# Opening of a two-block transformer kernel: loads, modulation, bounds and first norm in one stage, a ring of 12 modulation slots, every eighth group multiplied as plain fp32

## The chip, the cores and the metric

The kernel runs on one core of one Trainium2 chip. The metric is the device time of one execution in microseconds (us); lower is better. The kernel before took 4742.59 us (median of 3 runs, 4739.91 to 4749.90).

## What is computed

Two transformer blocks, one after the other, on 256 tokens of 1024 features in fp32. The first has two layers. Each layer modulates its normalised input by shift, scale and gate vectors which are products of a conditioning vector with a large weight matrix. These products, for the token stream and for a context stream, are the work that the change touches:

```python
cond_x = jax.nn.silu(c)
cond_c = jax.nn.silu(c_ctx)
for l in range(DEPTH):                                  # DEPTH = 2
    mod_x = (cond_x @ w_mod[l] + b_mod[l])[:, None, :]  # w_mod[l]: 1024 x 6144
    mod_c = (cond_c @ w_mod[l] + b_mod[l])[None, None, :]
    ...
    hc = modulate(rms_norm(xc, norm1_g[l]), sh1c, sc1c)
    ...
    hx = modulate(rms_norm(x, norm1_g[l]), sh1x, sc1x)
```

Here `modulate(h, shift, scale)` is `h * (1 + scale) + shift` and `rms_norm` divides by the root of the mean square over the features. `lower`, a softmax over the small `lb_logits`, gives the bounds of the forget gates. What follows in each layer (a gated linear recurrence with a short convolution, then a layer of 16384 experts of which 128 are gathered per token, then the second block) is the same in both kernels.

## The kernel before

Everything is written out by hand for each engine: a stage is a block in which SyncE (SP), TensorE (PE), ScalarE (ACT), VectorE (DVE) and GpSimd (POOL) each run their own list in order, and semaphores tie them. Between two stages all engines meet (`stage`, L124). The first stages, up to the first projection, are these:

1. **load** (L2761): SP issues the small tables, the constants, the tokens (`X`, 2 MB), and the first six weight units; it waits for all but the units.
2. **cond** (L577): ACT makes silu of both conditioning vectors and its rounded high part; DVE makes the low part (`parts`).
3. **modulate** (L597): the modulation weights of both layers are 96 units of 128x1024 fp32 (512 KB each), in 24 groups of four. They pass through the ring `k.ring` of 6 slots (`RING`). fp32 precision is reached with a faster matmul format by splitting each unit: ACT casts it to a high part (`w_high`, L645), DVE subtracts it from the unit to get a low part (`w_low`, L665), which also frees the ring slot: SP waits for it and then loads unit u + 6. For a group, PE multiplies 4 stationary columns (`parts`: high and low of two conditioning vectors) by 512 moving columns, 8 k-tiles x 2 parts = 16 matmuls (L629). ACT copies the 4x512 result out of PSUM (`rows`, L650), PE turns it by four small matmuls against the constant `fold` (`turn`, L617), and DVE adds the bias (`take`, L658). PE turns group g-1 after it has multiplied group g; ACT copies group g-1 after it has cast group g; DVE takes group g-2 after the subtractions of group g. `w_high` and `w_low` have room for two groups, so ACT may cast group g only when PE has multiplied group g-2:

```python
act.wait_ge(s.multiplied, g - 1)     # ahead of the casts of group g
act.wait_ge(s.multiplied, g)         # ahead of the copy of group g-1
```

4. **bounds** (L672): a load of the activation tables, then a chain of small DVE operations with one ACT exponential, on 128x8 and 128x16 values.
5. **w_in of layer 0** (`stream` L335, called from `token_mixer_1` L1134): first the norm. ACT squares the 8 tiles of `X` (L233), DVE adds them (7 additions, L261), PE sums over partitions with a matrix of ones (L254, with 16 and 14 filling matmuls before and after, L163), ACT takes Ln and Exp (L238, L240). Then tile by tile DVE scales (L268), ACT applies gain and shift (L248) and makes the high part (L457), DVE the low part (L501), and PE multiplies with the first weight unit (L416). From the second unit on the stage streams weight units, 24 matmuls each.

`Norm` (L212) holds the norm's steps for each engine. `Order` (L147) makes DVE wait for each of its own results.

Of the kernel before, what the change touches and what calls it, by code (L numbers as in the profile page):

```python
# [15 lines left out]
P = 128  # L16
D = 1024
# [156 lines left out]
def plan_weights(a):  # L174
# [7 lines left out]
    for l in range(DEPTH):  # L182
        chunks(a.w_mod[l], range(48))
    for l in range(DEPTH):
# [27 lines left out]
class Norm:  # L212
# [5 lines left out]
    def __init__(self, k, x, T, gain, shift, out):  # L218
        self.k, self.x, self.T, self.gain, self.shift, self.out = k, x, T, gain, shift, out
# [10 lines left out]

    def act_squares(self, act, s):
        for c in range(KD):
            act.activation(self.sq[:, c, :], self.x[:, c, :], ACT.Square).then_inc(s.squares, 1)  # L233
# [101 lines left out]
def stream(k, name, outs, x, evict, signals="", gain=None, norm=None, split_x=None, ahead=True, tables=False,  # L335
# [32 lines left out]
    with ExitStack() as es, stage(k, name, "x_high x_low took squares added sum logged root scaled shifted " + signals) as (block, s):  # L368
# [8 lines left out]
        if norm is not None:  # L377
            norm.place(es)
# [17 lines left out]
        def _(pe):  # L396
            steps = None
            if norm is not None:
                fill(k, pe, 16, 0)
                norm.pe_sum(pe, s)  # L400
                fill(k, pe, 14, 0)
            elif split_x is None:
                fill(k, pe, 4, 0)
            for u, (c, j) in enumerate(unit_of):
# [17 lines left out]
                if u == LAG:  # L422
                    if gain is not None or norm is not None:
                        pe.wait_ge(s.logged, 1)
# [9 lines left out]
        def _(act):  # L434
# [11 lines left out]
            if norm is not None:  # L446
                norm.act_squares(act, s)
            make(first + 1)
            if norm is not None:
# [28 lines left out]
        def _(dve):  # L478
# [11 lines left out]
            if norm is not None:  # L490
                norm.dve_add(dve, s)
            make(first + 1)
            if norm is not None:
                norm.dve_scale(dve, s, 0)
            if split_x is None:
                for t in range(KT):
                    if norm is not None and t + 1 < KT:
# [74 lines left out]
def modulation(k):  # L572

    with ExitStack() as es:
        cond = sbuf(k, es, "cond", [P, KD, 2])
        parts = sbuf(k, es, "parts", [P, KD, 2, 2], F32R)
        with stage(k, "cond", "done high") as (block, s):  # L577
            @block.scalar
            def _(act):

                act.activation(cond[:, :, 0], k.small("c_ctx"), ACT.Silu)
                act.activation(cond[:, :, 1], k.small("c"), ACT.Silu).then_inc(s.done, 1)
                act.wait_ge(s.done, 1)
                act.copy(parts[:, :, 0, :], cond[:, :, :]).then_inc(s.high, 1)

            @block.vector
            def _(dve):
                dve.wait_ge(s.high, 1)
                dve.tensor_tensor(parts[:, :, 1, :], cond[:, :, :], parts[:, :, 0, :].bitcast(F32), ALU.subtract)

        n_units, first = DEPTH * 48, k.used
        n_groups = n_units // 4
        k.used += n_units
        with stage(k, "modulate", "w_high w_low took turned added multiplied") as (block, s):  # L597
            rows = sbuf(k, es, "rows", [4, 2, 4 * P])
            w_high, w_low = (sbuf(k, es, n, [P, 2, 4, D], F32R) for n in ("w_high", "w_low"))
            fold = k.const("fold")[0:4, :]  # L600

            @block.sync
            def _(sp):
                for u in range(n_units):

                    sp.wait_ge(s.w_low, u + 1)
                    load_unit(k, sp, u + RING)

            @block.tensor
            def _(pe):  # L610
                def turn(g):

                    pe.wait_ge(s.took, g + 1)
                    if g >= 2:
                        pe.wait_ge(s.added, g - 1)
                    for i in range(4):
                        last = pe.matmul(k.bank[4 + g % 2][:, 2 * i:2 * i + 2], rows[:, g % 2, i * P:(i + 1) * P], fold,  # L617
                                         start=True, stop=True)
                    last.then_inc(s.turned, 1)

                for g in range(n_groups):
                    if g >= 4:

                        pe.wait_ge(s.took, g - 3)

                    pe.wait_ge(s.w_low, 4 * g + 4)
                    for t in range(KD):
                        for n_pass, w in enumerate((w_high, w_low)):
                            last = pe.matmul(k.bank[g % 4][0:4, :], parts[:, t, :, :].rearrange("p a b -> p (a b)"),  # L629
                                             w[:, g % 2, :, t * P:(t + 1) * P], start=(t == 0 and n_pass == 0), stop=(t == KD - 1 and n_pass == 1))  # L630
                    last.then_inc(s.multiplied, 1)
                    if g >= 1:
                        turn(g - 1)
                turn(n_groups - 1)

            @block.scalar
            def _(act):
                for g in range(n_groups + 1):
                    for u in range(4 * g, min(4 * g + 4, n_units)):
                        if g >= 2:  # L640

                            act.wait_ge(s.multiplied, g - 1)

                        act.wait_ge(k.landed[u % RING], 16 * (u // RING + 1))
                        act.copy(w_high[:, g % 2, u % 4, :], k.ring[:, u % RING, :]).then_inc(s.w_high, 1)  # L645
                    if g >= 1:
                        act.wait_ge(s.multiplied, g)
                        if g >= 3:
                            act.wait_ge(s.turned, g - 2)
# [2212 lines left out]
```

## Time and profile before

| what | value |
|---|---|
| median of 3 runs | 4742.59 us (4739.91 to 4749.90) |
| span of the profiled execution, first to last instruction | 4744.7 us |
| execution time of that same run | none is given beside its span |
| mean granted TensorE clock | 0.962 of full speed |
| busy share of the span: PE, DVE, ACT, POOL | 84%, 62%, 42%, 21% |
| modulate: first to last split matmul | 22.42 to 152.57 us |
| first matmul of the first projection | 171.62 us |

The span is the one measure in which the trace can be summed; the median lies 2.1 us under it. A matmul group is written line, engine, operation, output<-inputs. In rows of the timeline the first number is the start, the second how long the merged instructions took together. Idle time in square brackets is that of the engine just before, with what ended it.

### The profile page before, as it was taken

To read this page: it belongs to the slowest core of one execution; us is meant where nothing else is said; L and a number is where in the kernel's file an instruction comes from. 1 tells how busy PE (TensorE), PEld (TensorE's weight loads), DVE (VectorE), ACT (ScalarE), POOL (GpSimd) and SP (SyncE) were. 2 spreads that over 40 slices of the span, in tenths; PEclk is the share of its full clock that TensorE was granted. 3 is DMA by queue.
4 is the path that set the end of the run, shared out by engine and by line. 5 is a ranking of instruction groups with operands and counts; after the bars stand their busy time and mean duration, and the time that the engine had idled before them with its cause. 6 is when DMAs were issued, how large, how long until landed. Compare 5 with 4: busy or idle time off the path is not lost. (4 is left out here: it accounts for less than half of the span.)

```text
span 4744.7 us, 58234 instructions
## 1 busy us (share of the span) xinstructions
PE 3992.4 (84%) x20895; PEld 2891.1 (61%) x20895; DVE 2951.7 (62%) x6036; ACT 1989.0 (42%) x4530; POOL 987.2 (21%) x914
## 2 busy tenths in 40 slices
PE   7895897777777777796877777899989999999999
PEld 3685663223232232396632222789989988998899
DVE  7646556676666666566766665546566574565565
ACT  7635323333333333454333333544434353444453
POOL 0004114444444444203244443000010003000000
PEclk9997999999999999998999999989999998999999
DMA  9420149999999999631699999315534540254244
GB/s 371 168 89 1 54 178 421 421 421 418 413 415 413 414 415 415 261 131 39 256 421 422 419 412 410 111 54 171 160 99 147 162 147 18 77 168 148 81 152 151
DMA packets 205745, 1143.73 MB, mean 241 GB/s; under 512 B 24064, under 2 KB 25600, under 8 KB 106640
## 3 DMA queue, kind: packets, MB, share of 16 engines
q0 software_dynamic: 110592, 805.36, 41.1%
q1 hardware_dynamic: 94864, 334.65, 21.5%
q8 instruction: 166, 2.72, 0.2%
q14 instruction: 123, 1.01, 0.1%
HBM read 1138.87 MB, written 1.05 MB: 240 GB/s over the span
## 5 line engine op out<-in xcount | busy, mean ns | idle before, releaser
L1396 PE MATMUL bank<-rows,diag 128*128 128x512 f32 x2304 | 1080.8, 614 | 375.6 <-ACT diag L1455 375.6
L416 PE MATMUL bank<-x_high,w_high 128*128 128x272 f32 (+3 forms) x3560 | 1105.9, 311 | 20.5 <-DVE x_low L501 18.7
L416 PE MATMUL bank<-x_high,w_low 128*128 128x272 f32 (+3 forms) x3560 | 1086.3, 305 | 0.0
L416 PE MATMUL bank<-x_low,w_high 128*128 128x272 f32 (+3 forms) x3560 | 1084.2, 305 | 0.0
L1396 PEld LDWEIGHTS bank<-rows,diag 128*128 128x128 f32 x2304 | 422.4, 193 | 1027.4 <-ACT diag L1455 594.7
L1502 DVE CUSTOM_DVE_ANT_0 junk<-rows,hT 128x1024 f32<-128x1024 f32 x576 | 705.4, 1225 | 410.2 <-DMA rows<-in_peer_uv,expert 406.0
L443 ACT CAST w_high<-ring 128x1024 fp32r<-128x1024 f32 (+2 forms) x541 | 554.9, 1029 | 872.5 <-PE bank L416 859.4
L486 DVE TENSOR_TENSOR w_low<-ring,w_high 128x1024 fp32r<-128x1024 f32 (+2 forms) x541 | 647.3, 1198 | 334.5 <-ACT w_high L443 333.1
L1352 POOL DMA_INDIRECT rows<-in_peer_uv,expert x576 | 614.4, 1067 | 1108.8 <-PE bank L1396 806.7
L416 PEld LDWEIGHTS bank<-x_high,w_high 128*128 128x128 f32 (+1 forms) x3560 | 675.6, 190 | 64.0 <-DVE x_low L501 23.1
L416 PEld LDWEIGHTS bank<-x_low,w_high 128*128 128x128 f32 (+1 forms) x3560 | 676.6, 190 | 22.8
L416 PEld LDWEIGHTS bank<-x_high,w_low 128*128 128x128 f32 (+1 forms) x3560 | 675.3, 190 | 23.3
L1444 ACT ACTIVATE gelu<-products 128x2 f32<-128x2 f32 x384 | 78.1, 203 | 1277.7 <-DVE products L1502 1277.7
L1396 PE MATMUL bank<-H,diag 128*128 128x512 f32 x768 | 358.1, 609 | 120.1 <-ACT diag L1455 120.1
L1502 DVE CUSTOM_DVE_ANT_0 junk<-H,hT 128x1024 f32<-128x1024 f32 x192 | 235.3, 1225 | 211.5 <-DMA H<-in_peer_uv,expert 211.5
L1396 PEld LDWEIGHTS bank<-H,diag 128*128 128x128 f32 x768 | 139.5, 191 | 337.7 <-ACT diag L1455 197.2
L1455 ACT ACTIVATE diag<-const,weighed 128x128 f32<-128x128 f32 x768 | 266.8, 394 | 0.6 <-ACT weighed L1449 0.4
L1352 POOL DMA_INDIRECT H<-in_peer_uv,expert x192 | 190.0, 990 | 281.5 <-PE bank L1396 277.1
L416 PE MATMUL bank<-hidden_high,w_high 128*128 128x272 f32 (+1 forms) x704 | 202.2, 287 | 1.5 <-PEq L130 1.5
L416 PE MATMUL bank<-hidden_high,w_low 128*128 128x272 f32 (+1 forms) x704 | 201.7, 286 | 0.0
L416 PE MATMUL bank<-hidden_low,w_high 128*128 128x272 f32 (+1 forms) x704 | 201.5, 286 | 0.0
L1449 ACT ACTIVATE weighed<-gelu,weight 128x1 f32<-128x1 f32 x768 | 184.4, 287 | 15.5
(399 smaller groups left out, 4794.7 us busy)
## 6 DMA issues: line engine op xcount, KB each, us to landing
ring<-in_w_gate_up SPq DMA_DIRECT2D x176, 512.0 KB, 3.5
ring<-in_w_mod SPq DMA_DIRECT2D x96, 512.0 KB, 5.5
ring<-in_w_in SPq DMA_DIRECT2D x64, 512.0 KB, 3.5
ring<-in_fox_w_in SPq DMA_DIRECT2D x64, 512.0 KB, 3.5
ring<-in_w_down SPq DMA_DIRECT2D x64, 512.0 KB, 3.5
ring<-in_peer_wq SPq DMA_DIRECT2D x32, 512.0 KB, 3.5
ring<-in_gdn_w_in SPq DMA_DIRECT2D x32, 512.0 KB, 3.5
ring<-in_w_down SPq DMA_DIRECT2D x32, 384.0 KB, 3.7
```

Of the source, the lines that this page charges most:

```text
L416: last = pe.matmul(k.bank[c % outs_banks][0:m, 0:nt], w[:, slot, cols], xx[:, t, t0:t0 + nt], start=(t == 0 and n_pass == 0), stop=(t == K ...
L443: act.copy(k.w_high[:, made % SPLIT, 0:width(made)], k.ring[:, made % RING, 0:width(made)]).then_inc(k.high_made, 1)
L486: dve.tensor_tensor(k.w_low[:, made % SPLIT, 0:n], k.ring[:, made % RING, 0:n], k.w_high[:, made % SPLIT, 0:n].bitcast(F32), ALU.subtract) ...
L1352: pool.indirect_dma_start(slot(n), None, table, bass.IndirectOffsetOnAxis(ap=expert[:, i % 2, e:e + 1], axis=0)).then_inc(landed[n % SLOTS ...
L1396: last = pe.matmul(k.bank[2 * (i % 2) + half][:, :], diag[:, n % 4, :], slot(n)[:, D + half * 512:D + (half + 1) * 512], start=(e == 0), s ...
L1444: act.activation(gelu[:, pair % 4, :], products[:, i % 2, e:e + 2], ACT.Gelu).then_inc(s.gelu, 1)
L1449: act.mul(weighed[:, pair % 4, j:j + 1], gelu[:, pair % 4, j:j + 1], weight[:, i % 2, e + j:e + j + 1]).then_inc(s.weighed, 1)
L1455: act.mul(diag[:, (n + j) % 4, :], k.ident, weighed[:, pair % 4, j:j + 1]).then_inc(s.diag, 1)
L1502: dve.tensor_tensor_reduce(junk[:, n % 2, :], slot(n)[:, 0:D], hT[:, i, :], 1.0, 0.0, ALU.mult, ALU.add, products[:, i % 2, e:e + 1]).then ...
```

## The change

The first four stages and the norm of the first projection become one stage, `opening`.

- SP issues the table `small`, then 12 modulation units into a ring of their own (`MOD_RING`), then the other five tables, then the tokens, then the remaining 84 units, and at last the first six units of the projection weights into `k.ring`.
- Groups 7, 15 and 23 are `whole`: no cast and no subtraction; PE multiplies them straight out of the ring by `cond` in fp32, 8 matmuls of 2 stationary and 512 moving columns, and their slots are freed when the group is multiplied. The other 21 groups are split as before, with the same two places for `w_high` and `w_low`.
- PE waits for all five tables before its first group. ACT squares two tiles of `X` after each of the groups 3 to 6 and takes the root after group 11's place; DVE adds the squares after the subtractions of group 8, scales two tiles in each of the groups 13 to 16, and makes the bounds at group 1; PE sums at group 9.
- The projection stage then starts with gain and shift; its filling matmuls are 10.

The diff, without the removed stages (they stand in the kernel above), the small operations on 128x8 values, and the plumbing:

```diff
-            act.wait_ge(s.scaled, c + 1)
+            if not self.scaled:
+                act.wait_ge(s.scaled, c + 1)
...
-        if norm is not None:
+        rooted = norm is not None and not norm.scaled
+        if rooted:
             norm.place(es)
...
-            if norm is not None:
+            if rooted:
                 fill(k, pe, 16, 0)
                 norm.pe_sum(pe, s)
                 fill(k, pe, 14, 0)
+            elif norm is not None:
+                fill(k, pe, 10, 0)
...
+MOD_RING = 12
+WHOLE_EVERY = 8
+def opening(k, a, norm):
+    n_units = DEPTH * 48
+    n_groups = n_units // 4
+    whole = lambda g: g % WHOLE_EVERY == WHOLE_EVERY - 1
+    wholes = lambda g: g // WHOLE_EVERY
+    halved = lambda u: u + 1 - 4 * wholes(u // 4)
+    side = lambda g, first, last: range(max(0, KD * (g - first) // (last - first)), min(KD, KD * (g - first + 1) // (last - first)))
+    signals = ("small tables tokens landed0 landed1 landed2 landed3 landed4 landed5 landed6 landed7 landed8 landed9 landed10 landed11 "
+               "done high parts w_high w_low took turned biased multiplied order exps subs ")
+    with ExitStack() as es, stage(k, "open", signals + norm.signals) as (block, s):
+        landed = [s.landed0, s.landed1, s.landed2, s.landed3, s.landed4, s.landed5, s.landed6, s.landed7, s.landed8, s.landed9,
+                  s.landed10, s.landed11]
...
+        @block.sync
+        def _(sp):
+            def load(u):
+                sp.dma_start(ring[:, u % MOD_RING, :], a.w_mod[u // 48][u % 48]).then_inc(landed[u % MOD_RING], 16)
+            sp.dma_start(k.small_sb[:, :], a.small).then_inc(s.small, 16)
+            for u in range(MOD_RING):
+                load(u)
+            for dst, src in ((k.const_sb[:, :], a.const), (k.both[:, :, :], a.both), (k.fox_b[:, :], a.fox_b),
+                             (k.gdn_ab[:, :], a.gdn_ab), (k.alpha[:, :], a.gla_w_alpha2_2[0])):
+                sp.dma_start(dst, src).then_inc(s.tables, 16)
+            sp.dma_start(k.X[:, :, :], a.tokens).then_inc(s.tokens, 16)
+            for u in range(n_units - MOD_RING):
+                if whole(u // 4):
+                    sp.wait_ge(s.multiplied, u // 4 + 1)
+                else:
+                    sp.wait_ge(s.w_low, halved(u))
+                load(u + MOD_RING)
+            for u in range(RING):
+                load_unit(k, sp, u)
+        @block.tensor
+        def _(pe):
+            def turn(g):
+                pe.wait_ge(s.took, g + 1)
+                if g >= 2:
+                    pe.wait_ge(s.biased, g - 1)
+                n = 2 if whole(g) else 4
+                for i in range(4):
+                    last = pe.matmul(k.bank[4 + g % 2][:, 2 * i:2 * i + 2], rows[0:n, g % 2, i * P:(i + 1) * P], fold[0:n, :],
+                                     start=True, stop=True)
+                last.then_inc(s.turned, 1)
+            pe.wait_ge(s.parts, 1)
+            pe.wait_ge(s.tables, 16 * 5)
+            for g in range(n_groups):
+                if g >= 4:
+                    pe.wait_ge(s.took, g - 3)
+                if whole(g):
+                    at = 4 * g % MOD_RING
+                    for u in range(4 * g, 4 * g + 4):
+                        pe.wait_ge(landed[u % MOD_RING], 16 * (u // MOD_RING + 1))
+                    for t in range(KD):
+                        last = pe.matmul(k.bank[g % 4][0:2, :], cond[:, t, :], ring[:, at:at + 4, t * P:(t + 1) * P],
+                                         start=(t == 0), stop=(t == KD - 1))
+                else:
+                    pe.wait_ge(s.w_low, halved(4 * g + 3))
                     for t in range(KD):
                         for n_pass, w in enumerate((w_high, w_low)):
                             last = pe.matmul(k.bank[g % 4][0:4, :], parts[:, t, :, :].rearrange("p a b -> p (a b)"),
+                                             w[:, split_group(g) % 2, :, t * P:(t + 1) * P], start=(t == 0 and n_pass == 0),
+                                             stop=(t == KD - 1 and n_pass == 1))
+                last.then_inc(s.multiplied, 1)
+                if g >= 1:
+                    turn(g - 1)
+                if g == 9:
+                    norm.pe_sum(pe, s)
+            turn(n_groups - 1)
+        @block.scalar
+        def _(act):
...
+            before = {}
+            for g in range(n_groups):
+                if not whole(g):
+                    before[split_group(g)] = g
+            for g in range(n_groups + 1):
+                if g < n_groups and not whole(g):
+                    j = split_group(g)
                     for u in range(4 * g, 4 * g + 4):
+                        if j >= 2:
+                            act.wait_ge(s.multiplied, before[j - 2] + 1)
+                        act.wait_ge(landed[u % MOD_RING], 16 * (u // MOD_RING + 1))
+                        act.copy(w_high[:, j % 2, u % 4, :], ring[:, u % MOD_RING, :]).then_inc(s.w_high, 1)
+                if g >= 1:
+                    act.wait_ge(s.multiplied, g)
+                    if g >= 3:
+                        act.wait_ge(s.turned, g - 2)
+                    n = 2 if whole(g - 1) else 4
+                    act.copy(rows[0:n, (g - 1) % 2, :], k.bank[(g - 1) % 4][0:n, :]).then_inc(s.took, 1)
+                if g == 3:
+                    act.wait_ge(s.tokens, 16)
+                for c in side(g, 3, 7):
+                    norm.act_square(act, s, c)
+                if g == 11:
+                    norm.act_root(act, s)
         @block.vector
         def _(dve):
             order = Order(dve, s.order)
+            lb = k.small("lb_logits").rearrange("p (l n) -> p l n", l=DEPTH)
+            def take(g):
+                dve.wait_ge(s.turned, g + 1)
+                l, c = divmod(4 * g, 48)
+                bias = k.small("b_mod")[:, 4 * g:4 * g + 4].unsqueeze(2).broadcast_to([P, 4, 2])
+                dve.tensor_tensor(k.mods[:, l, c:c + 4, :], k.bank[4 + g % 2][:, 0:8].rearrange("p (c q) -> p c q", q=2),
+                                  bias, ALU.add).then_inc(s.biased, 1)
                 for n, (scale0, name) in enumerate(((8, "norm1_g"), (32, "norm2_g"))):
+                    if c == scale0 + 4:
+                        dve.wait_ge(s.biased, g + 1)
+                        gain = k.small(name)[:, l * KD:(l + 1) * KD].unsqueeze(2).broadcast_to([P, KD, 2])
+                        dve.scalar_tensor_tensor(out=k.gain[:, l, n, :, :], in0=k.mods[:, l, scale0:scale0 + KD, :],
+                                                 scalar=1.0, in1=gain, op0=ALU.add, op1=ALU.mult)
...
+            dve.wait_ge(s.high, 1)
+            dve.tensor_tensor(parts[:, :, 1, :], cond[:, :, :], parts[:, :, 0, :].bitcast(F32), ALU.subtract).then_inc(s.parts, 1)
+            for g in range(n_groups):
+                if not whole(g):
+                    j = split_group(g)
+                    for u in range(4 * g, 4 * g + 4):
+                        dve.wait_ge(s.w_high, halved(u))
+                        dve.tensor_tensor(w_low[:, j % 2, u % 4, :], ring[:, u % MOD_RING, :], w_high[:, j % 2, u % 4, :].bitcast(F32),
+                                          ALU.subtract).then_inc(s.w_low, 1)
+                if g >= 2:
+                    take(g - 2)
+                if g == 1:
+                    dve.wait_ge(s.exps, 1)
...
+                if g == 8:
+                    norm.dve_add(dve, s)
+                for c in side(g, 13, 17):
+                    norm.dve_scale(dve, s, c)
+            take(n_groups - 2)
+            take(n_groups - 1)
 def first_block(k, a):
-    modulation(k)
...
-            token_mixer_1(k, l, Norm(k, k.X[:, :, :], TWO, gain(0), shift(0), k.H[:, :, :]))
+            token_mixer_1(k, l, Norm(k, k.X[:, :, :], TWO, gain(0), shift(0), k.H[:, :, :], scaled=(l == 0)))
...
+        norm = Norm(k, k.X[:, :, :], TWO, None, (), k.H[:, :, :])
+        with ExitStack() as first:
+            norm.place(first)
+            opening(k, a, norm)
```

Four pieces of the engines' order show the move. The names are the lines of each kernel.

PE around group 7. Before:

```order
L629 MATMUL bank<-w_low,parts 4x512
L617 MATMUL bank<-const,rows 128x2 x4
L629 MATMUL bank<-w_high,parts 4x512
L629 MATMUL bank<-w_low,parts 4x512
L629 MATMUL bank<-w_high,parts 4x512
```

and now (L651 is the multiplication of a whole group, L636 the turn of the group before it):

```order
L657 MATMUL bank<-w_low,parts 4x512
L636 MATMUL bank<-const,rows 128x2 x4
L651 MATMUL bank<-mod_ring,cond 2x512 x8
L636 MATMUL bank<-const,rows 128x2 x4
L657 MATMUL bank<-w_high,parts 4x512
L657 MATMUL bank<-w_low,parts 4x512
```

In place of 16 split matmuls stand 8 of plain fp32, and the turn of group 6 comes behind them.

DVE in groups 6 to 9. Before, subtractions and one bias addition alternate:

```order
L665 TENSOR_TENSOR w_low<-ring,w_high 128x1024 x4
L658 TENSOR_TENSOR mods<-bank,small 128x8
L665 TENSOR_TENSOR w_low<-ring,w_high 128x1024 x4
L658 TENSOR_TENSOR mods<-bank,small 128x8
L665 TENSOR_TENSOR w_low<-ring,w_high 128x1024 x4
```

and now:

```order
L736 TENSOR_TENSOR w_low<-mod_ring,w_high 128x1024 x4
L713 TENSOR_TENSOR mods<-bank,small 128x8 x2
L736 TENSOR_TENSOR w_low<-mod_ring,w_high 128x1024 x4
L713 TENSOR_TENSOR mods<-bank,small 128x8
L263 TENSOR_TENSOR total<-H 128x512
L263 TENSOR_TENSOR total<-total,H 128x512 x6
L736 TENSOR_TENSOR w_low<-mod_ring,w_high 128x1024 x4
L713 TENSOR_TENSOR mods<-bank,small 128x8
```

The seven additions of the norm stand behind the bias addition of group 6 (the last L713 ahead of them) and in front of the subtractions of group 9.

## Rows read from the trace of the kernel before

**Rows 1.** Windows: busy us of each engine, clock, DMA share, GB/s
```profile
core 0: us, PE busy (x) PEld busy (x) DVE busy (x) ACT busy (x) POOL busy (x), PEclk, DMA share, GB/s
23.00:149.00 126.00, 114.23 (x544) 51.89 (x541) 111.03 (x114) 102.23 (x113) 0.00 (x0) 0.97 0.99 380
```
**Rows 2.** Groups by line and shape, 14 to 160 us
```profile
L665 DVE TENSOR_TENSOR w_low<-ring,w_high 128x1024 fp32r<-128x1024 f32 x96 | 114.3, 1222 | 13.2 <-ACT w_high L645 10.9
L645 ACT CAST w_high<-ring 128x1024 fp32r<-128x1024 f32 x96 | 98.0, 1045 | 15.3 <-DMA ring<-in_w_mod 13.6 <-PEq L130 0.5 <-PE bank L629 0.2
```
**Rows 3.** Timeline of two groups that no load held up: ACT, DVE, PE
```profile
94.81 0.57 ACT L650 COPY rows<-bank 4x512 f32<-4x512 f32 x1 [1.81 <-PE bank L629]
95.30 3.89 ACT L645 CAST w_high<-ring 128x1024 fp32r<-128x1024 f32 x4
...
96.37 4.63 DVE L665 TENSOR_TENSOR w_low<-ring,w_high 128x1024 fp32r<-128x1024 f32 x4 [0.41 <-ACT w_high L645]
...
101.14 0.39 PE L629 MATMUL bank<-w_high,parts 128*4 128x512 f32 x1 [0.62 <-DVE w_low L665]
...
104.61 0.39 PE L629 MATMUL bank<-w_low,parts 128*4 128x512 f32 x1
104.94 1.05 PE L617 MATMUL bank<-const,rows 4*128 4x2 f32 x8
...
105.04 0.57 ACT L650 COPY rows<-bank 4x512 f32<-4x512 f32 x1 [0.31 <-PE bank L629]
```
**Rows 4.** Timeline: PE's first matmul of groups 0, 2 and 23
```profile
22.42 0.59 PE L629 MATMUL bank<-w_high,parts 128*4 128x512 f32 x1 [22.42 <-DVE w_low L665]
...
34.13 0.40 PE L629 MATMUL bank<-w_high,parts 128*4 128x512 f32 x1 [1.61 <-DVE w_low L665]
...
149.10 0.39 PE L629 MATMUL bank<-w_high,parts 128*4 128x512 f32 x1 [0.28 <-DVE w_low L665]
```
**Rows 5.** Timeline: end of modulate (DVE), first squares (ACT)
```profile
154.88 0.17 DVE L658 TENSOR_TENSOR mods<-bank,small 128x8 f32<-128x8 f32 x1 [0.73 <-PE bank L617]
...
159.02 4.27 ACT L233 ACTIVATE H<-X 128x512 f32<-128x512 f32 x8 [2.18 <-PEq L130]
```
**Rows 6.** Timeline: the norm, up to the first projection matmul
```profile
161.01 4.67 DVE L261 TENSOR_TENSOR total<-total,H 128x512 f32<-128x512 f32 x6
...
167.61 0.63 ACT L240 ACTIVATE total<-total 128x512 f32<-128x512 f32 x1
...
168.28 1.29 DVE L268 TENSOR_TENSOR H<-X,total 128x512 f32<-128x512 f32 x2 [1.47 <-ACT total L240]
...
169.00 1.09 ACT L248 ACTIVATE H<-H,mods,gain 128x256 f32<-128x256 f32 x2 [0.76 <-DVE H L268]
...
171.62 0.47 PE L416 MATMUL bank<-x_high,w_high 128*128 128x512 f32 x1 [1.64 <-DVE x_low L501]
```
**Rows 7.** Timeline in the experts: plain fp32 matmuls of 512 columns, two records each
```profile
708.28 3.70 PE L1396 MATMUL bank<-rows,diag 128*128 128x512 f32 x8 [1.16 <-ACT diag L1455]
```
**Rows 8.** Windows, columns as in rows 1: clock and load rate
```profile
56.00:60.00 4.00, 4.00 (x12) 1.25 (x11) 3.95 (x4) 3.03 (x3) 0.00 (x0) 0.58 0.97 358
...
140.00:144.00 4.00, 3.37 (x20) 1.69 (x18) 3.81 (x5) 3.54 (x5) 0.00 (x0) 1.00 1.02 408
...
156.00:160.00 4.00, 0.96 (x4) 0.99 (x5) 1.54 (x10) 1.81 (x4) 0.00 (x0) 0.50 0.00 0
...
840.00:880.00 40.00, 29.86 (x66) 11.61 (x65) 27.71 (x74) 13.24 (x44) 16.16 (x16) 1.00 1.01 422
```
**Rows 9.** Timeline: PE matmuls when the granted clock was low
```profile
91.58 0.63 PE L629 MATMUL bank<-w_high,parts 128*4 128x512 f32 x1
92.01 0.63 PE L629 MATMUL bank<-w_low,parts 128*4 128x512 f32 x1
```
**Rows 10.** DMA issues: KB each, median us from issue to landing
```profile
ring<-in_w_in SPq DMA_DIRECT2D x64, 512.0 KB, 3.5
...
const<-in_const SPq DMA_DIRECT2D x1, 1113.0 KB
```

More of the change, by code:

```diff
@@ L496, in _ @@
                 for t in range(KT):
-                    if norm is not None and t + 1 < KT:
+                    if rooted and t + 1 < KT:
                         norm.dve_scale(dve, s, t + 1)
@@ L594, in modulation @@
[L594 to L626, printed above, removed]
@@ new lines, in opening @@
+        ring = sbuf(k, es, "mod_ring", [P, MOD_RING, D])
+        rows = sbuf(k, es, "rows", [4, 2, 4 * P])
+        w_high, w_low = (sbuf(k, es, n, [P, 2, 4, D], F32R) for n in ("w_high", "w_low"))
+        top = sbuf(k, es, "top", [P, 8])
+        e = sbuf(k, es, "e", [P, DEPTH, 8])
+        total = sbuf(k, es, "total", [P, 8])
+        fold = k.const("fold")
+        split_group = lambda g: g - wholes(g)
+        @block.sync
[17 more added lines that the diff above has]
+                load_unit(k, sp, u)
@@ L629, in _ @@
                             last = pe.matmul(k.bank[g % 4][0:4, :], parts[:, t, :, :].rearrange("p a b -> p (a b)"),
[L630 to L649, printed above, removed]
-                        act.copy(rows[:, (g - 1) % 2, :], k.bank[(g - 1) % 4][0:4, :]).then_inc(s.took, 1)
@@ L672, in modulation @@
-    with ExitStack() as es, stage(k, "bounds", "order exps subs") as (block, s):
-        lb = k.small("lb_logits").rearrange("p (l n) -> p l n", l=DEPTH)
-        top = sbuf(k, es, "top", [P, 8])
-        e = sbuf(k, es, "e", [P, DEPTH, 8])
-        total = sbuf(k, es, "total", [P, 8])
+                                             w[:, split_group(g) % 2, :, t * P:(t + 1) * P], start=(t == 0 and n_pass == 0),
+                                             stop=(t == KD - 1 and n_pass == 1))
+                last.then_inc(s.multiplied, 1)
@@ new lines, in _ @@
+                if g >= 1:
[5 more added lines that the diff above has]
+        def _(act):
+            act.wait_ge(s.small, 16)
+            act.activation(cond[:, :, 0], k.small("c_ctx"), ACT.Silu)
+            act.activation(cond[:, :, 1], k.small("c"), ACT.Silu).then_inc(s.done, 1)
+            act.wait_ge(s.done, 1)
+            act.copy(parts[:, :, 0, :], cond[:, :, :]).then_inc(s.high, 1)
+            load_tables(act)
+            act.wait_ge(s.subs, 2)
+            act.activation(e[:, :, :], e[:, :, :], ACT.Exp).then_inc(s.exps, 1)
+            before = {}
[5 more added lines that the diff above has]
+                    j = split_group(g)
+                    for u in range(4 * g, 4 * g + 4):
+                        if j >= 2:
[14 more added lines that the diff above has]
+                    norm.act_root(act, s)
```

94 lines of the change are left out of this document (22 added, 72 removed).

## The prediction

> **What bounds the stretch now.** Only the first 172 us change, so I read those: first the windows (which engine is full), then the groups by line (what each operation costs and waits for), then the timeline of a few groups (which loop sets the pace), then its ends. What comes after the first projection matmul is the same work and should move with it as a whole.
>
> In modulate no engine rests: in 126 us PE is busy 114.2, DVE 111.0, ACT 102.2, and the DMA engines run at a share of 0.99 with 380 GB/s [rows 1]. So three limits lie close together. For loads alone, a unit of 512 KB at the 408 GB/s that a good stretch of this stage shows [rows 8] takes 1.285 us, a group 5.14 us. PE's first matmul of group 2 starts at 34.13 and of group 23 at 149.10 [rows 4]: 114.97 us for 21 groups, 5.47 each. ACT stood 13.6 us in all waiting for loads, DVE 10.9 for ACT [rows 2].
>
> The third limit is a loop through three engines. ACT copies group g-1 when it is multiplied, then casts group g+1, DVE follows one unit behind, PE starts group g+1 when the last subtraction is done. The rows show one turn that no load held up: copy at 94.81, casts from 95.30, subtractions 96.37 to 101.00, PE from 101.14 to its last matmul at 104.61, next copy at 105.04 [rows 3]. That is 10.23 us, and as the two places of `w_high` let two such loops run side by side, **5.12 us per group**. Loads at their best and the loop thus ask for the same; the reader is to see that a deeper ring cannot go below 5.12. PE alone needs 3.47 us (101.14 to 104.61) and, from its last matmul over the turn to the next group, 0.33 and about 1.0: 4.8 us.
>
> **The change, part by part.**
>
> *Start.* The first units are now ahead of the tables, so ACT and DVE prepare groups 0 and 1 early. It brings nothing: PE waits for all tables (it needs only `fold` of them), behind 12 units. Ahead of PE are 12 x 512 KB of units, 1113 of `const` [rows 10], and by their shapes 512 of `both`, 182 of `small` and 32 of `alpha`: 8.17 MB, at 408 GB/s 20.0 us. A single unit takes 3.5 us from issue to landing [rows 10] and 1.3 of them for its bytes, so 2.2 us come on top; with some 1.3 us until the first issue (an estimate) PE begins at 23.5 us, against 22.42 [rows 4]. Group 2 can be cast only once group 0 is multiplied, so it moves too: **+1.3 us** at group 2. The bounds at group 1, nine operations of the size that takes 0.17 us [rows 5], fall where DVE waits for this anyway: nothing, and some 1.6 us if that wait were gone.
>
> *The ring of 12.* It takes away load waits. 5.47 less 5.12 is 0.35 us per group, 7.5 us over 21 groups; two falls of the clock in this stretch (below) cost PE 1.4 us each and are to be expected again, which leaves about **-5 us**. DVE and ACT then stand for 0 us by loads.
>
> *Whole groups.* Four plain fp32 matmuls of 512 columns appear as 8 records in 3.70 us [rows 7]; less the tail of the last, (3.70-0.59)/7 = 0.444 per record, 0.89 per matmul. Eight of them take 7.1 us, where a split group's 16 take 3.7. With the turn, PE needs 8.4 us for such a group, and no other engine can shorten that. Step by step: 8.4 for the whole group, then 4.8 for the next, which is ready by then, in place of 2 x 5.12: +3.0. Twice in this stretch (7 and 15): **+5.9 us**. The saved 4 casts and 4 subtractions hide nothing that bounds.
>
> *The norm inside.* Squares: two of 0.53 us (4.27/8 [rows 5]) after the copies of groups 2 to 5 lie in front of casts, half of each counts as two loops run side by side: 3 x 1.07 / 2 = **+1.6**; those before the whole group are hidden. Additions: at group 8 DVE first waits for the turn of group 6, which PE does only after the 7.1 us of group 7, and then adds for 5.4 us (4.67 for six [rows 6]); only then come the subtractions of group 9. After the end of group 7: 1.3 + 0.2 + 5.4 + 4.85 gives a start of group 9 at 11.7 us, where the loop alone would give 6.3; PE's sum (0.96) follows ahead of group 10: together **+5.9**. Behind DVE's additions are queued the slots of the ring, too, but 12 slots and loads that are faster than the loop cover that; without that cover a load wait of the same 5 us would follow. The root on ACT (Ln and Exp, 0.7 + 0.6 [rows 6]) stands ahead of casts: **+0.7**. The scaling, 1.3 us of DVE per group in 13, 14 and 16 (in 15 DVE is free): DVE's own round becomes 4.85 + 0.3 + 1.3 = 6.4, over 5.12 by 1.3; much of it is gone by the free group: **+1.7**.
>
> Sum from group 2 to group 23: -5 + 5.9 + 1.6 + 5.9 + 0.7 + 1.7 = **+10.8**.
>
> *End.* From the first matmul of group 23 to the last bias it took 155.04 - 149.10 = 5.9 us [rows 4, 5]; whole, it is 7.1 + 2.3 = 9.4: **+3.5**.
>
> *Between the stages.* Before: 155.04 to 171.62, 16.6 us for bounds, squares, additions, sum and root [rows 5, 6]. Now: 0.5 for the meeting of the engines, a cast of 1.0 [rows 2], and 2.62 from the first shift to the first projection matmul (169.00 to 171.62 [rows 6]): 4.1. **-12.5 us.** After that, ACT's shift and high part pace the tiles as before; the missing scaling on DVE was hidden.
>
> *Clock.* While the granted clock is 0.58 [rows 8] matmuls follow each other by 0.43 us, not 0.23 [rows 9]: level 1.2 against 2.4 GHz. After 4 us without work (155 to 159) it read 0.50 [rows 8]. Ahead of group 9 PE will now idle for 6 us; at 1.2 GHz the whole group costs 16 x 0.2 = 3.2 us more. I take half: **+1.5**.
>
> Sum: 1.3 + 10.8 + 3.5 - 12.5 + 1.5 = **+4.6 us**. Against the profiled span 4744.7 that is 4749.3; the runs' median lies 2.1 under the span, so 4742.6 + 4.6 = **4747.2 us**.
>
> **Rivals.**
>
> *A, loads set the end.* If casts and subtractions no longer pace the loop (shorter durations with fewer stalls), the 54.3 MB ahead of the last unit take 133 us at 408 GB/s, the last lands at 136, 9.4 us of group 23 and 4.1 follow: first projection matmul at 149.7, -21.9: **4720.7**. For it: load waits are the only waits of ACT that the groups show. Against: the turn in rows 3 held no load wait and still took 10.23 us. The experts reach 422 GB/s [rows 8]. The Trainium skill (DMA: Bandwidth & Descriptors, Measured) gives 425 GB/s for long streams on one core and only 341 for single 1 MB transfers; by its 425 the last unit would land 5 us sooner still, and the experts' rows agree with it.
>
> *B, the middle keeps its pace.* Whole groups, squares and additions all fit in slack (PE's and DVE's 10%), and the stage ends 3.5 us later only by its last group: 155.04 + 3.5 + 4.1 = 162.6, -9.0: **4733.6**. For it: each engine's total falls or hardly grows. Against: the additions stand in order in front of group 9.
>
> *C, the clock.* The idle ahead of group 9 sends the clock to 1.2 GHz, and the waits of 1.5 us that come at every second group keep it there. Each such group adds 3.2 us, wholly in the loop. It decides from four groups on (9 to 12): +12.8 in place of my 1.5, **4758.5**. Against: waits of 1.6 us before did not drop it (34.13 starts at 0.40 per record [rows 4]). The Trainium skill (TensorE: Matmul & The Clock Gate, HAM oscillation) describes just this: repeated waits between groups of matmuls keep sending the clock down; this trace shows it only for the longer pause.
>
> The early start failing to reach PE is no rival but part of the sum.
>
> **Numbers.** About 0.2% (9.5 us) is what a measurement of this kernel can tell from no change. Forecast 0.50, A 0.12, B 0.20, C 0.15, others 0.03. Faster: A and a third of B, which lies on the bound, 0.18. Slower: C and a little of the rest, 0.18. Within: 0.64. The range goes from a little under B to C, 4732 to 4759: it leaves out A and the far side of C.
>
> **What would show it.** PE's first group near 23.5 and group 2 near 35.4 us (without the tables' wait: 10 us earlier). Whole groups: 8 x 2 records of 0.44. A gap of 10 to 12 us between the starts of groups 8 and 9 with DVE in L263. ACT without DMA waits after group 2, DMA share under 0.95 in the middle. Last bias near 170 us, first projection matmul near 174 (176 with the clock's part); 150 would be A, 163 B, 187 C. I am wrong if the starts of split groups follow by less than 5.1 us on average, or if anything after the first projection changes by over 3 us.

## The result, and the profile after

The changed kernel takes 4759.51 us (median of 7 runs, 4754.13 to 4766.18) against 4742.59 for the kernel before (7 runs): ratio 1.0035, 95% interval 1.0025 to 1.0045. It is slower by 16.6 us by the ratio. In a later comparison on one chip the same code gave 1.0022 (1.0009 to 1.0034), 10.4 us. The profiled execution spans 4757.3 us, 12.6 more than before.

| where | before | after | difference | cumulative |
|---|---|---|---|---|
| PE's first matmul of group 2 | 34.13 | 37.46 | +3.3 | +3.3 |
| first matmul of group 2 to that of group 23 | 114.97 | 131.85 | +16.9 | +20.2 |
| group 23 to the end of the last bias | 5.94 | 9.11 | +3.2 | +23.4 |
| last bias to first projection matmul | 16.58 | 4.32 | -12.3 | +11.1 |
| first projection matmul to ACT's last `diag` in the first block's experts | 2798.8 | 2796.3 | -2.5 | +8.6 |
| from there to the end (the second block) | 1774.3 | 1778.3 | +4.0 | +12.6 |

The first four rows are the change. The last two are work that is the same in both; between executions they vary by several us either way (below), so I read the experiments at the first projection matmul and take the total from the runs.

Windows of the changed kernel (busy us of each engine, instructions, granted clock, DMA share, GB/s):

```profile
23.00:169.00 146.00, 127.10 (x544) 53.24 (x545) 100.01 (x115) 90.24 (x109) 0.00 (x0) 0.92 0.86 333
60.00:80.00 20.00, 17.56 (x72) 6.77 (x72) 10.86 (x16) 11.67 (x16) 0.00 (x0) 1.00 0.55 200
80.00:84.00 4.00, 0.00 (x0) 0.00 (x0) 4.00 (x5) 2.54 (x3) 0.00 (x0) 0.59 1.02 409
84.00:88.00 4.00, 2.97 (x8) 0.89 (x9) 4.00 (x5) 0.00 (x0) 0.00 (x0) 0.50 1.03 411
120.00:140.00 20.00, 18.69 (x73) 6.95 (x71) 14.20 (x18) 13.10 (x15) 0.00 (x0) 0.93 0.49 191
```

Against [rows 1], the DMA share has fallen from 0.99 to 0.86, and around the whole groups (7 and 15) to half; ACT and DVE have more rest than before (90 and 100 of 146 us). Loads are no limit any more, and what they left was not used. The clock fell from 0.97 to 0.92.

Groups by line and shape of the same kernel, 5 to 179 us, and two rows of its waits (us in total, times, longest):

```profile
L736 DVE TENSOR_TENSOR w_low<-mod_ring,w_high 128x1024 fp32r<-128x1024 f32 x84 | 97.7, 1219 | 23.7 <-ACT w_high L690 23.2
L690 ACT CAST w_high<-mod_ring 128x1024 fp32r<-128x1024 f32 x84 | 82.1, 1041 | 2.5 <-DMA mod_ring<-in_w_mod 2.5
L657 PE MATMUL bank<-w_high,parts 128*4 128x512 f32 x168 | 72.9, 434 | 41.9 <-DMA alpha<-in_gla_w_alpha 25.3 <-DVE w_low L736 16.6
```
```profile
ACT rows L696 <- PE bank L657: 55.3, 17, 14.8
PE bank L657 <- DVE w_low L736: 16.6, 9, 5.9
```

Beside [rows 2]: a cast and a subtraction cost what they did (1041 and 1219 ns), ACT's 13.6 us of load waits are 2.5, and a split matmul went from 409 to 434 ns on average, which is the clock. Timeline of PE and DVE from group 7 to group 9, and the start:

```profile
25.31 0.59 PE L657 MATMUL bank<-w_high,parts 128*4 128x512 f32 x1 [25.31 <-DMA alpha<-in_gla_w_alpha]
...
37.46 0.40 PE L657 MATMUL bank<-w_high,parts 128*4 128x512 f32 x1 [1.67 <-DVE w_low L736]
...
66.33 7.03 PE L651 MATMUL bank<-mod_ring,cond 128*2 128x512 f32 x16
73.29 1.05 PE L636 MATMUL bank<-const,rows 4*128 4x2 f32 x8
74.27 0.40 PE L657 MATMUL bank<-w_high,parts 128*4 128x512 f32 x1
...
78.08 1.05 PE L636 MATMUL bank<-const,rows 2*128 2x2 f32 x8
85.03 0.59 PE L657 MATMUL bank<-w_high,parts 128*4 128x512 f32 x1 [5.90 <-DVE w_low L736]
85.42 0.63 PE L657 MATMUL bank<-w_low,parts 128*4 128x512 f32 x1
85.84 0.63 PE L657 MATMUL bank<-w_high,parts 128*4 128x512 f32 x1
```
```profile
74.38 0.17 DVE L713 TENSOR_TENSOR mods<-bank,small 128x8 f32<-128x8 f32 x1 [2.73 <-PE bank L636]
74.46 0.68 DVE L263 TENSOR_TENSOR total<-H 128x512 f32<-128x512 f32 x1
75.25 0.69 DVE L263 TENSOR_TENSOR total<-total,H 128x512 f32<-128x512 f32 x1
76.47 3.88 DVE L263 TENSOR_TENSOR total<-total,H 128x512 f32<-128x512 f32 x5 [0.52 <-DVE total L263]
80.26 4.62 DVE L736 TENSOR_TENSOR w_low<-mod_ring,w_high 128x1024 fp32r<-128x1024 f32 x4
```

This is the forecast jam: DVE waits for the turn of group 6 behind the whole group, adds from 74.46 to 80.26, subtracts until 84.9, and PE starts group 9 at 85.03, 10.76 us after group 8, with an idle 5.90. What was not priced in full stands in the last PE rows: the matmuls then follow by 0.42 us, not 0.23. An interval of this kind is called slow below, and a stretch of them inside a group a fall of the clock. Of the intervals between neighbouring split matmuls after group 2, 41 are slow, in groups 4, 9, 12, 14 and 17; before there were 15, in groups 6 and 12.

### The profile page after: what moved, and what is told of

Read it like the earlier page. It is cut to its first block and busy times, and to the rows that moved or that the text cites. A ratio compares the mean times of both kernels' runs of the same rounds, so it can differ in the third digit from the quotient of the medians.

```text
span 4757.3 us, 57983 instructions
## 1 busy us (share of the span) xinstructions
PE 4011.0 (84%) x20855; PEld 2894.7 (61%) x20855; DVE 2935.2 (62%) x6024; ACT 1973.7 (41%) x4518; POOL 988.9 (21%) x914
```

## The experiments

The measure is the first projection matmul: 171.62 us before, 182.74 changed. Each time at it is read from one profiled execution; two executions of the kernel before stand 2.2 us apart there, two of the changed one 0.5. Ratios are to the kernel before, with intervals. In the edits, `...` stands for lines that are left out.

**x1_no_whole.** No whole groups.
```diff
-WHOLE_EVERY = 8
+WHOLE_EVERY = 1000
```


> The change with all 24 groups split (no group multiplied as plain fp32). Read at the first projection matmul (L421), which stands at 182.74 us in the changed kernel and 171.62 before. Theory (PE is held by the whole groups: 7.9 + 4.8 us for a whole group and its successor where two split ones take 10.2): -2.5 us for each of groups 7 and 15, -3.3 for group 23, less about 1.3 because DVE now also has group 15's subtractions beside the norm's scaling: first projection matmul at 176 to 177, total near 4753. Rival (whole groups relieve ACT and DVE, which are what bounds): later than 182.7, up to 190, total over 4760.

174.75 us, 8.0 earlier; total 1.0014 (1.0004 to 1.0024). The whole groups cost about 8 us; the rival that they relieve ACT and DVE to a gain has fallen. It is 1.3 to 2.3 us more than I expected.

**x2_norm_outside.** The norm back in the projection stage.
```diff
-                if g == 9:
-                    norm.pe_sum(pe, s)
...
-                for c in side(g, 3, 7):
-                    norm.act_square(act, s, c)
-                if g == 11:
-                    norm.act_root(act, s)
...
-                if g == 8:
-                    norm.dve_add(dve, s)
-                for c in side(g, 13, 17):
-                    norm.dve_scale(dve, s, c)
...
-            token_mixer_1(k, l, Norm(k, k.X[:, :, :], TWO, gain(0), shift(0), k.H[:, :, :], scaled=(l == 0)))
+            token_mixer_1(k, l, Norm(k, k.X[:, :, :], TWO, gain(0), shift(0), k.H[:, :, :]))
```


> The change with the norm of the first projection left where it was before (squares, additions, sum, root and scaling in the projection stage), all else as changed. Theory (the norm inside costs in the stage about what it saves behind it, since its additions keep PE waiting ahead of group 9 and its scaling slows DVE): last bias of the stage 12 to 15 us earlier than 178.4, the gap to the first projection matmul 12.7 instead of 4.3 us; first projection matmul at 176 to 179, total 4753 to 4756. Rival (hiding the norm is the gain of the change and something else costs): first projection matmul at 188 or later, total over 4764.

173.66 us; total 1.0004 (0.9989 to 1.0019). Its last bias ends at 160.4, 18.0 us earlier than in the changed kernel, and the gap to the projection is 13.3, 8.9 us longer. So the norm inside, with the falls of the clock that come with it, costs 18 us to save 9. After group 2 no matmul is slow. Its windows, and its last bias:

```profile
40.00:130.00 90.00, 86.09 (x398) 37.12 (x396) 68.07 (x77) 63.52 (x73) 0.00 (x0) 1.00 0.90 358
```
```profile
160.24 0.17 DVE L705 TENSOR_TENSOR mods<-bank,small 128x8 f32<-128x8 f32 x1 [0.73 <-PE bank L636]
```

**x3_const_first.** The constants ahead of the units, PE waiting for them alone.
```diff
             sp.dma_start(k.small_sb[:, :], a.small).then_inc(s.small, 16)
+            sp.dma_start(k.const_sb[:, :], a.const).then_inc(s.consts, 16)
...
-            pe.wait_ge(s.tables, 16 * 5)
+            pe.wait_ge(s.consts, 16)
...
```


> The change with the constants loaded right behind the small table and PE waiting for them alone. Theory (the early units bring nothing because PE waits for the tables until 25.3 us): PE's first matmul at about 14 us instead of 25.3, all of it kept since loads have slack in the middle (DMA share 0.5 in two windows of 20 us): first projection matmul at 172, total near 4749. Rival (loads bound the stage once PE is early): the last bias moves by 5 us or less, first projection matmul at 177 or later, ACT shows load waits of over 5 us in all.

PE starts at 14.55, but the projection only at 176.33, where I had 172: 10.8 us gained at the start, 6.4 kept; total 1.0006 (0.9996 to 1.0016). ACT waits 9.7 us for units in all, which was the rival's sign, and its longest wait stands in these rows:

```profile
24.86 0.57 ACT L698 COPY rows<-bank 4x512 f32<-4x512 f32 x1
30.17 1.05 ACT L692 CAST w_high<-mod_ring 128x1024 fp32r<-128x1024 f32 x1 [4.74 <-DMA mod_ring<-in_w_mod]
```

Group 3's first unit is queued behind the tables and the 2 MB of tokens, and now it is reached before it has landed: group 3 starts 9.5 us after group 2, against 4.8 in the changed kernel.

**x4_fill.** Filling matmuls in PE's wait ahead of group 9.
```diff
+                if g == 9:
+                    fill(k, pe, 44, 6)
```


> The change with 44 filling matmuls of 128 columns on a free PSUM bank in PE's wait ahead of group 9. Theory (PE idle for 5.9 us ahead of group 9 is why its 16 matmuls follow by 0.43 us): they follow by 0.23 us, group 9 takes 3.5 instead of 6.2 us, first projection matmul 2.5 to 3 us earlier, 180. Rival (the clock falls whatever PE does): group 9 keeps 0.43 us in most of its matmuls, or a fall of the same length stands in a neighbouring group, and the first projection matmul stays at 182 to 184.

No interval of group 9 or of its neighbours is slow (they are 0.23 us), but the projection starts at 183.33; total 1.0026 (1.0014 to 1.0038). The filling took 10.1 us where 5.9 were free, and group 9 starts 14.62 us after group 8, not 10.76, so what the clock gave back was lost again. The first half of the theory holds, the time was a miss of my own sizing. Elsewhere the falls stood in other groups than in the changed kernel: in 6, 14 and 17, with 24 slow intervals in all. Ahead of group 9 both kernels do the same work, and yet the fall in group 4 is not there and group 6 has one:

```profile
49.60 0.39 PE L659 MATMUL bank<-w_high,parts 128*4 128x512 f32 x1 [1.66 <-DVE w_low L738]
...
60.87 0.40 PE L659 MATMUL bank<-w_high,parts 128*4 128x512 f32 x1 [1.10 <-DVE w_low L738]
...
62.15 0.63 PE L659 MATMUL bank<-w_high,parts 128*4 128x512 f32 x1
62.58 0.63 PE L659 MATMUL bank<-w_low,parts 128*4 128x512 f32 x1
```

**e5_ring_only.** x1 and x2 together: no whole groups, norm outside.

> The change without whole groups and with the norm left in the projection stage: what stays is the merging of loads, modulation and bounds, the ring of 12, and the tables behind the first units. Theory (the two costs are separate: 8.0 us for the whole groups, 9.0 for the norm inside, as measured one by one): first projection matmul at 182.7 - 8.0 - 9.0 = 165.7, groups following by 5.12 us with no fall of the clock after group 2; total about 4737 to 4739. Rival (each only matters while the other is there): 171 or later.

163.38 us, 2.3 earlier than the two costs added; total 0.9995 (0.9983 to 1.0008). From group 2 to 23 it takes 107.1 us, 5.10 per group, with no slow matmul and loads at 408 GB/s:

```profile
40.00:130.00 90.00, 84.44 (x425) 39.82 (x423) 83.91 (x92) 76.71 (x89) 0.00 (x0) 1.00 1.03 408
```

The loop of [rows 3] sets the pace here: a group starts 4.77 and 5.46 us after the last, in turn, and ACT waits 0.7 us for loads in all (its row stands with e6_ring6). The loads run at 408 GB/s, which I had taken as their best, so the two limits still lie close together.

**e6_ring6.** The same with a ring of 6.
```diff
-MOD_RING = 12
+MOD_RING = 6
```


> As e5_ring_only, with the modulation ring cut to 6 slots. Theory (the deeper ring removes the load waits that stood in the kernel before, 5.47 against 5.12 us per group): groups at 5.3 to 5.5 us, ACT waits for loads over 8 us in all, first projection matmul 5 to 7 us later than in e5_ring_only. Rival (the depth brings nothing, the waits of before came from elsewhere): within 1.5 us of e5_ring_only.

169.87 us, 6.5 later; total 0.9997 (0.9980 to 1.0013), which the totals don't tell from e5. From group 2 to 23 it takes 117.4 us, 5.59 per group, with 23 slow intervals: 10.3 us more than e5, of which some 4.6 (23 x 0.2) are clock. Group 2 starts 3.8 us earlier, since only six units stand ahead of the tables, so 6.5 are left at the projection. The wait that comes back (ACT for loads, from 13 us on; the longest is at the start):

```profile
ACT w_high L688 <- DMA mod_ring<-in_w_mod: 22.1, 40, 9.4
```
and in e5_ring_only:
```profile
ACT w_high L688 <- DMA mod_ring<-in_w_mod: 0.7, 3, 0.2
```

**e7_early_late.** e5 with the constants behind the first four units, the other tables and the tokens last.
```diff
             for u in range(MOD_RING):
+                if u == 4:
+                    sp.dma_start(k.const_sb[:, :], a.const).then_inc(s.consts, 16)
                 load(u)
...
```


> As e5_ring_only, with the constants loaded behind the first four units, PE waiting for them alone, and the other tables and the tokens loaded behind the last modulation unit. Theory (PE's start was held by the tables, and group 3 in x3_const_first by the tokens and tables queued ahead of its units): PE's first matmul at 13 to 15 us, group 23 starts 21 x 5.12 after group 2, first projection matmul at 153 to 156, total about 4727. Rival (loads bound once the start is early): ACT waits for loads over 8 us, first projection matmul at 159 or later.

PE starts at 13.70 and the projection at 153.65, 18.0 us before that of the kernel before, and groups follow by 5.10 us again. The total is 0.9981 (0.9969 to 0.9993), 9 us faster: less than 18, but clear of no change.

```profile
13.70 0.59 PE L659 MATMUL bank<-w_high,parts 128*4 128x512 f32 x1 [13.70 <-DMA const<-in_const]
```

**e8_spread.** e7's early constants, tokens behind unit 15, and the norm inside but one step per group.
```diff
-                if g == 8:
-                    norm.dve_add(dve, s)
-                for c in side(g, 13, 17):
+                if 6 <= g <= 12:
+                    norm.dve_add_one(dve, s, g - 5)
+                for c in side(g, 16, 24):
...
```


> No whole groups, constants early as in e7_early_late, tokens behind unit 15, and the norm inside the stage but spread out: one square in each of groups 3 to 10, one addition in 6 to 12, sum at 13, root at 15, one scaling in 16 to 23. Theory (the norm costs DVE 0.7 us in each of 15 groups, above its 4.9 of 5.12, about 8 us, and saves 8.4 behind the stage): first projection matmul within 2 us of e7_early_late. Rival (it was only the lump ahead of group 9 that cost; spread out the norm hides): 5 us or more earlier than e7_early_late.

154.27 us, 0.6 from e7_early_late, as the theory had it; total 0.9981 (0.9969 to 0.9994). Spread out, the norm inside costs about what it saves; in a lump it cost 9 us net beside whole groups (x2_norm_outside) and 11.4 without them (x1_no_whole to e5_ring_only). The pair e7 and e8 isn't clean, though: e8 also loads the tokens early, PE waits 3.03 us ahead of group 4, and the clock falls in groups 2 and 4, none of which e7 has.

**f1_before_again and f2_after_again.** Both kernels once more.

> The kernel before once more, to see how far one profiled execution stands from another. Theory (up to the first projection the trace repeats itself within 2 us, the second block does not): first projection matmul at 170 to 173 us; from the last diag of the experts to the end 1774 to 1786 us. If the second block gives 1774 again while the later experiments stand at 1784 to 1786, their longer second block is theirs and not the chip's.

> The changed kernel once more. Theory (the falls of TensorE's clock follow PE's waits): again 3 to 6 groups after group 2 in which matmuls follow by 0.43 us, group 9 among them, each behind a wait of over 1 us; first projection matmul at 180 to 184. Rival (the falls are chance): they stand in other groups, also behind waits of 0.6 us or less, and the count differs by half.

The kernel before: projection at 173.83 (+2.2, a little outside what I gave; three falls of the clock, in groups 2, 6 and 12, where there were two), total 1.0002 (0.9990 to 1.0014). The changed kernel: 183.27 (+0.5), its slow intervals in groups 4, 9, 12, 14 and 17 again, some 41 of them. So they follow the waits of over a us; none stands behind a wait of 0.6 us or less. But which of these waits ends in a fall isn't fixed: up to group 6, x1_no_whole and x4_fill do the same work as the changed kernel, and the clock fell in groups 2, 4 and 6 of the one and in group 6 alone of the other. The parts behind the projection vary too: the second block took 1774 and 1781 us in two executions of the kernel before, 1778 and 1775 in two of the changed one, 1775 to 1778 in x1 to x4, 1784 to 1786 in e5 to e8, 1783 in f4 below. What makes these ten us is open: f4 ran on one chip with f2 and f3 (1778), and e6, only 1.8 us ahead of the kernel before at the projection, has them too. The ratios of e7 and e8 are 8 to 9 us short of what their first 172 us gained.

**f3_fill_all.** Filling that fits, in six waits.
```diff
+                if g in (4, 6, 9, 12, 14, 17):
+                    fill(k, pe, 22 if g == 9 else 5, 6)
```


> The change with filling matmuls in PE's waits: 22 ahead of group 9 (44 took 10.1 us, too long for the wait of 5.9), 5 ahead of each of groups 4, 6, 12, 14 and 17. Theory (the waits cause the falls): at most one fall of the clock left after group 2, which takes 6 to 8 us of the 41 slow matmuls away, first projection matmul at 174.5 to 177. Rival (falls come anyway): three or more falls, first projection matmul at 180 or later.

174.20 us, 8.5 earlier than the changed kernel and 9.1 earlier than in f2_after_again; total 1.0013 (1.0004 to 1.0023). Not one slow interval is left from group 2 on. The timeline at group 9, and the windows there:

```profile
77.69 5.18 PE L163 MATMUL bank<-const 128*128 128x128 f32 x44
83.66 0.39 PE L659 MATMUL bank<-w_high,parts 128*4 128x512 f32 x1 [0.79 <-DVE w_low L738]
83.89 0.40 PE L659 MATMUL bank<-w_low,parts 128*4 128x512 f32 x1
```
```profile
80.00:84.00 4.00, 3.21 (x28) 2.88 (x27) 4.00 (x6) 1.28 (x2) 0.00 (x0) 1.00 1.02 417
84.00:88.00 4.00, 4.00 (x21) 1.66 (x19) 4.00 (x4) 0.45 (x1) 0.00 (x0) 1.00 1.02 410
```

Group 9 still starts 10.74 us after group 8, so there filling changed nothing but the clock: 1.00 where it was 0.59 and 0.50. That PE's waits cause the falls is shown by this. It does not show which waits do.

**f4_spread_late.** e8 with the tokens behind unit 27 and the norm's steps two or three groups later. The edit is shown against e8.
```diff
-                if u == 3:
+                if u == 15:
                     sp.dma_start(k.X[:, :, :], a.tokens).then_inc(s.tokens, 16)
...
```


> As e8_spread, with the tokens loaded behind unit 27 instead of 15 and the norm's steps moved back: squares in groups 6 to 13, additions 8 to 14, sum at 15, root at 17, scaling in 18 to 23. Theory (in e8_spread group 4 waited 3 us for units queued behind the tokens): that wait goes, first projection matmul at 150 to 152.5, total 0.2 to 0.3% under the kernel before. Rival (the 2 MB of the tokens have to be loaded in any case and the wait only moves): 154 or later.

158.13 us: the rival holds. ACT now waits for the tokens themselves and then for the units behind them, ahead of and in the casts of group 7, which starts 8.50 us after group 6:

```profile
49.94 0.63 ACT L230 ACTIVATE H<-X 128x512 f32<-128x512 f32 x1 [1.86 <-DMA X<-in_tokens]
```

Its total is 0.9974 (0.9961 to 0.9987), 12 us faster; by the intervals it is not told apart from e7 and e8. Any of the three beats both kernels, by 0.2 to 0.3% against the kernel before.

## Why the prediction was wrong

Forecast +4.6 us, in a range that ended at 4759.0; measured 4759.5 by the median, which is 16.9 us more. At the first projection matmul, where the sum was made, it is +11.1 against +4.6.

- *What bounds.* Right. With load waits gone and nothing added (e5_ring_only), groups follow by 5.10 us; I had 5.12 from one turn of the loop. That is why rival A did not come.
- *Ring of 12.* Right. In the middle it is worth 10.3 us, 5.7 without the clock (e5, e6); I had 5, the two falls of before set aside.
- *Whole groups.* +5.9 and +3.5, 9.4 in all. Right: 7.03 us for eight matmuls, and group 8 started 7.94 after group 7, where I had 8.4; taking them out gives 8.0 (x1), and 10.3 where the norm is outside (x2 to e5).
- *End, and between the stages.* +3.2 and -12.3, against +3.5 and -12.5. Right.
- *Start.* Mis-sized: "**+1.3 us** at group 2" was 3.3. The last of the tables, `alpha`, landed at 25.2 and not at 23.5. From 8 to 24 us the windows show 401 to 424 GB/s, which is my rate, but from 4 to 8 us it was 379 and before that 122. That the early units bring nothing was right.
- *Norm inside.* The jam ahead of group 9, its order and its length were right (10.76 us between the starts of 8 and 9, forecast 10 to 12). So was the sum of the terms: from group 2 to 23, f3_fill_all, where no matmul is slow, takes 123.3 us, and x2_norm_outside, without its fall in group 2, about 112.6. That leaves 10.7 for the norm against 9.9. What the waits did to the clock was not in it.
- *Clock.* This step failed: "I take half: **+1.5**". Beside the two falls of before I priced one, at group 9, and ruled out others by one row ("waits of 1.6 us before did not drop it"). Five came, 26 slow intervals of 0.2 us more than before, 5.2 us. The norm's steps on ACT and DVE lengthen PE's short waits from 0.6 (x2_norm_outside) to between 1.3 and 1.9 us, and behind these the clock fell. f3_fill_all takes all of it away and gets 8.5 us. One wait that cost nothing was no proof: in f1_before_again the very same wait, 1.60 us ahead of group 2, did end in a fall. And the trace of before already said otherwise. It has four waits of over a us after group 1, ahead of groups 2, 6, 12 and 18, and two of them, of 1.28 and 1.12 us, end in falls; so it is not so that "this trace shows it only for the longer pause":

```profile
55.78 0.40 PE L629 MATMUL bank<-w_high,parts 128*4 128x512 f32 x1 [1.28 <-DVE w_low L665]
...
57.20 0.63 PE L629 MATMUL bank<-w_low,parts 128*4 128x512 f32 x1
57.63 0.63 PE L629 MATMUL bank<-w_high,parts 128*4 128x512 f32 x1
...
89.35 0.40 PE L629 MATMUL bank<-w_high,parts 128*4 128x512 f32 x1 [1.12 <-DVE w_low L665]
```

Rival C had the mechanism, only with the falls in groups 9 to 12 and 12.8 us for them. That the measured total is its 4758.5 to about a us is luck: at the projection it gives 187 and 182.7 was measured, and the rest came behind it. The Trainium skill (TensorE: Matmul & The Clock Gate, HAM oscillation) tells of waits between tiles of matmuls that send the clock down at every tile, there behind load waits longer than most of the waits here. The runs agree in part: with the waits filled (f3) no fall was left, but waits as long ahead of groups 2 and 6 of the changed kernel brought none.

Middle, summed: +16.9, against 10.8 + 1.5. The 4.6 us between are 3.7 of the clock and 0.9 left over.

At the projection the change is 11.1 us; the first ratio gives 16.6 (11.9 to 21.3 by its interval), the second 10.4 (4.3 to 16.1). What stands between 11.1 and 16.6 has no cause shown. My own sign of being wrong, that anything behind the projection changes by over 3 us, came up (+4.0 in the second block), but it was a bad sign: two executions of the kernel before differ by 7 us there.

## What to carry to other kernels

When several engines pass a group of work round in a loop with two buffers, a stage has a floor of its own beside that of its loads: find it in a turn without load waits, and price each operation that is put in by the engine and the place in that loop where it stands. A short serial stage hidden inside such a loop in one piece stalled the loop, and TensorE's stall cost a second time through the clock; cut into pieces it cost about what it saved (e8_spread), so no run here shows that hiding it pays. When you forecast the clock, count every long wait of the trace before and what followed it, not one. Before loads are reordered, ask what the first consumer waits for: here one table of 1.1 MB, moved up while the other tables and the tokens moved back, brought the projection 9.7 us forward (e5 to e7), more than the 6.5 of the ring (e6 to e5).

## What the runs showed of the hardware

- The granted clock fell behind PE waits of 0.9 to 5.9 us (0.90 in f1, 5.90 in the changed kernel); in the 21 groups after group 2 of e5, with waits of at most 0.62 us, it never fell. Not each longer wait did it: in the changed kernel 1.66 us ahead of group 4 did and the same ahead of group 6 did not, in x4_fill neither the 1.66 us ahead of group 4 nor the 1.86 us ahead of group 12 did, but 1.10 us ahead of group 6 did.
- Matmuls of a constant on a free bank held the clock at 1.00 through a wait of 5.9 us (f3). Each of 128 columns in fp32 takes about 0.23 us (5.18 us for 22 in f3), so 44 of them are 10.1 us (x4): they have to be counted.
- A plain fp32 matmul of 512 columns with 2 stationary columns cost about as much as with 128: 0.43 us per record, two records each (7.03 us for 8 in the changed kernel), against 0.44 in [rows 7].
